# Attention probabilities transposed in 32x32 blocks by VectorE, weighted sums on four row groups of TensorE

## The reference, cut to what matters

```python
def attend(qb):                       # one block of 128 queries
    s = jnp.einsum('bqgrd,bkgd->bgrqk', qb, k).astype(jnp.float32)
    p = jax.nn.softmax(s, axis=-1).astype(v.dtype)
    return jnp.einsum('bgrqk,bkgd->bqgrd', p, v)
```

## Time and profile before

| what | value |
|---|---|
| median of 3 runs | 1152.69 us (1152.6 to 1153.32) |
| the profiled execution's own time | 1152.85 us |
| its span, first to last instruction | 1151.1 us |
| PE busy | 99% of the span |
| DVE busy | 54% |
| ACT busy | 40% |
| POOL busy | 7% |
| mean granted TensorE clock | 0.999 |

### The profile page before, as it was taken

The page is one execution under the profiler, slowest core; times in us unless marked ns, Lnnn a source line. Parts: engine busy times, 40 slices in busy tenths (PEclk is TensorE's granted clock), DMA queues, the critical chain, the costliest instruction groups (busy, mean ns, idle before and its releaser), DMA issues.

```text
span 1151.1 us, 16031 instructions
## 1 busy us (share of the span) xinstructions
PE 1142.1 (99%) x6071; PEld 922.3 (80%) x6071; DVE 620.0 (54%) x776; ACT 455.4 (40%) x682; POOL 83.6 (7%) x74
## 2 busy tenths in 40 slices
PE   9999999999999999999999999999999999999997
PEld 7888888888888777666788888888888888888886
DVE  6755555553332684444598857655455555542223
ACT  6423223232222446455767655434423223232223
POOL 0000000000001120000054320020000000000000
PEclk9999999999999999999999999999999999999999
DMA  6332232332323341211121212432232232232221
GB/s 206 110 109 91 91 109 91 99 126 101 100 86 122 131 132 60 73 56 56 55 93 57 75 56 92 165 102 100 92 110 91 91 109 90 92 105 96 92 92 73
DMA packets 31679, 111.59 MB, mean 97 GB/s; under 512 B 3984, under 2 KB 5136, under 8 KB 31376
## 3 DMA queue, kind: packets, MB, share of 16 engines
q1 hardware_dynamic: 30192, 104.11, 26.9%
q10 hardware_dynamic: 1440, 6.82, 1.6%
HBM read 105.41 MB, written 4.19 MB: 95 GB/s over the span
## 4 chain that ended last, share of the span: by engine, by line
PE 99%; DMA 0%; DVE 0%; ACT 0%; issue 0%; ACTq 0%; DVEq 0%
PE ps L1161 27%; PE ps L1163 26%; PE ps L1162 26%; PE ps L1196 3%; PE ps L1195 3%; PE ps L1197 3%; PE ps L1301 1%; PE ps L1312 1%; PE ps L1327 1%; PE ps L1456 1%; PE ps L1432 1%; PE ps L1410 0%; PE ps L1449 0%; DMA raw<-up_dram 0%; PE ps L1361 0%; PE ps L1234 0%
## 5 line engine op out<-in xcount | busy, mean ns | idle before, releaser
L1161 PE MATMUL ps<-h_hi,w_hi 128*128 128x512 f32 x1024 | 407.4, 398 | 0.0
L1163 PE MATMUL ps<-h_hi,w_lo 128*128 128x512 f32 x1024 | 399.0, 390 | 0.0
L1162 PE MATMUL ps<-h_lo,w_hi 128*128 128x512 f32 x1024 | 398.8, 389 | 0.0
L768 DVE TENSOR_TENSOR w_lo<-raw,w_hi 128x1024 fp32r<-128x1024 f32 (+2 forms) x190 | 234.4, 1236 | 191.2 <-ACT w_hi L414 185.0
L414 ACT ACTIVATE w_hi<-raw 128x1024 fp32r<-128x1024 f32 (+1 forms) x182 | 196.3, 1080 | 168.0 <-PE ps L1163 96.2
L1161 PEld LDWEIGHTS ps<-h_hi,w_hi 128*128 128x128 f32 x1024 | 192.2, 188 | 55.5 <-issue 15.6
L1162 PEld LDWEIGHTS ps<-h_lo,w_hi 128*128 128x128 f32 x1024 | 192.3, 188 | 41.4 <-issue 2.9
L1163 PEld LDWEIGHTS ps<-h_hi,w_lo 128*128 128x128 f32 x1024 | 192.2, 188 | 40.5
L484 ACT ACTIVATE g_hi<-un 128x512 f32 (+1 forms) x44 | 27.8, 632 | 250.8 <-DVE un L768 250.8
L768 DVE TENSOR_TENSOR un<-ps,rs 128x512 f32<-128x512 f32 x44 | 30.4, 691 | 122.2 <-PE ps L1163 122.2
L1161 PE MATMUL ps<-g_hi,w_hi 128*128 128x512 f32 x176 | 68.5, 389 | 0.0
(11 more groups left out here) (241 smaller groups left out, 1189.8 us busy)
## 6 DMA issues: line engine op xcount, KB each, us to landing
raw<-up_dram SPq DMA_DIRECT2D x86, 512.0 KB, 3.2
raw<-proj_dram SPq DMA_DIRECT2D x26, 512.0 KB, 3.2
raw<-down_dram SPq DMA_DIRECT2D x16, 704.0 KB, 4.0
raw<-down_dram SPq DMA_DIRECT2D x22, 512.0 KB, 3.2
raw<-gates_dram SPq DMA_DIRECT2D x16, 512.0 KB, 3.2
raw<-branch_dram SPq DMA_DIRECT2D x8, 512.0 KB, 3.2
raw<-wout_dram SPq DMA_DIRECT2D x8, 512.0 KB, 3.3
x_spill_dram<-xT ACTq DMA_DIRECT2D x1, 2048.0 KB, 7.2
```

Source lines behind the costliest of these rows:

```text
L768: return V.tensor_tensor(out, a, b, op)
L1161: T.matmul(ps[:, bank, :], w_hi[:, slot, cols], moving_hi(j), start=start and j == 0, stop=False)
L1162: T.matmul(ps[:, bank, :], w_hi[:, slot, cols], moving_lo(j), start=False, stop=False)
L1163: ins = T.matmul(ps[:, bank, :], w_lo[:, slot, cols], moving_hi(j), start=False, stop=stop and j == tiles - 1)
```

## The change

The 128x128 transposes by PE and the copies behind them go. Instead DVE transposes `prob` in 32x32 blocks within each group of 32 partitions (`prob_blocks`: one instruction of 512 elements per partition and two of 256). A block transpose leaves the queries' group of 32 where it was, so partitions 32i to 32i + 31 now hold, for queries 32i to 32i + 31, all 512 keys in 16 blocks of 32. The weighted sum therefore contracts over 32 keys at a time in each of the four row groups, with the values of every key block copied to all four groups (`v_rep`, by 32 new DMAs on SP). The result of row group i goes to PSUM bank 4 + i, and `y_hi` and `y_lo` gather it from four banks.

```diff
+BLOCK = 32
+BLOCKS = S // BLOCK
+QUADS = P // BLOCK
...
+        v_rep = [at("v_rep0", 80, [P, BLOCKS // 2, P]), at("v_rep1", 100, [P, BLOCKS // 2, P])]
...
-        UP_BANKS, RES_BANKS, MEAN_BANK, Y_BANKS = (0, 2), 4, 6, (6, 7)
+        UP_BANKS, RES_BANKS, MEAN_BANK, Y_BANK = (0, 2), 4, 6, 4
...
+                        if FIRST_ITEM <= i < FIRST_ITEM + QUADS:
+                            to = i - FIRST_ITEM
+                            if to == 0:
+                                sp.wait_ge(vn_done, 1)
+                            for half in range(2):
+                                for quad in range(QUADS):
+                                    sp.dma_start(v_rep[half][BLOCK * to:BLOCK * (to + 1), quad::QUADS, :],
+                                                 v_a[BLOCK * quad:BLOCK * (quad + 1), 2 * half:2 * half + 2, :]).then_inc(vrep_loaded, 16)
                         sp.wait_ge(lo_done, BASE[name] + i + 1)
...
-            def prob_t_copy(q):
-                act.wait_ge(pt_done, 2 * q + 1)
...
-                A(prob_t0[:, :, q % 4, :], ps[:, 4, :].rearrange("p (j c) -> p j c", c=P), ACT.Copy).then_inc(pta_done, 1)
...
+            def prob_blocks(q):
+
+                if q == 0:
+                    dve.wait_ge(spilled, 16)
+                elif q % 4 == 0:
+                    dve.wait_ge(pv_done, q // 4)
+                dve.wait_ge(pn_done, 2 * q + 1)
+                V.transpose(prob_t0[:, :, q % 4, :], prob[:, 0, :].rearrange("p (j c) -> p j c", c=BLOCK)).then_inc(pt_done, 1)
+                dve.wait_ge(pn_done, 2 * q + 2)
+                for half in range(2):
+                    V.transpose(prob_t1[half][:, :, q % 4, :],
+                                prob[:, 1, S // 2 * half:S // 2 * (half + 1)].rearrange("p (j c) -> p j c", c=BLOCK)).then_inc(pt_done, 1)
+
             def attention_step(q):
 
                 if 0 <= q - 1 < ITEMS:
-                    dve.wait_ge(pt_done, 2 * q)
...
-                    for half in range(2):
-                        V.tensor_copy(prob_t1[half][:, :, (q - 1) % 4, :],
-                                      ps[:, 5, S // 2 * half:S // 2 * (half + 1)].rearrange("p (j c) -> p j c", c=P)).then_inc(ptb_done, 1)
+                    prob_blocks(q - 1)
...
-            def prob_transposes(q):
...
             def weighted(t):
                 if t == 0:
-                    pe.wait_ge(vn_done, 1)
-                if t == 1:
+                    pe.wait_ge(vrep_loaded, 16 * 2 * QUADS * QUADS)
+                    pe.wait_ge(qeps_done, 5)
                     pe.wait_ge(vn_done, 5)
...
+                else:
+                    pe.wait_ge(yalo_done, t)
+                pe.wait_ge(pt_done, 12 * t + 12)
+                for j in range(BLOCKS):
+                    for i in range(QUADS):
+                        keys = slice(BLOCK * i, BLOCK * (i + 1))
+                        for a, rows in enumerate(head_rows):
+                            probs = prob_t1[j // 8][keys, j % 8, :, :] if a else prob_t0[keys, j, :, :]
+                            ins = T.matmul(ps[rows, Y_BANK + i, P * t:P * (t + 1)], v_rep[j // 8][keys, j % 8, rows],
+                                           probs.rearrange("p s c -> p (s c)"), start=j == 0, stop=j == BLOCKS - 1)
...
             def key_transposes(u):
                 pe.wait_ge(ke_done, u + 1)
+                if u == 0:
+                    pe.wait_ge(yalo_done, PAIRS)
```

More of the change, by code:

```diff
@@ L154, in build @@
         prob = at("prob", 76, [P, 2, S])
-        prob_t0 = nc.alloc_sbuf_tensor_at("prob_t0", [P, ST, 4, P], F32, offset=big_at + 2 * 4 * S)
-        prob_t1 = [nc.alloc_sbuf_tensor_at("prob_t1a", [P, ST // 2, 4, P], F32, offset=big_at + 6 * 4 * S),
-                   at("prob_t1b", 56, [P, ST // 2, 4, P])]
+        prob_t0 = nc.alloc_sbuf_tensor_at("prob_t0", [P, BLOCKS, 4, BLOCK], F32, offset=big_at + 2 * 4 * S)
+        prob_t1 = [nc.alloc_sbuf_tensor_at("prob_t1a", [P, BLOCKS // 2, 4, BLOCK], F32, offset=big_at + 6 * 4 * S),
+                   at("prob_t1b", 56, [P, BLOCKS // 2, 4, BLOCK])]
+        v_rep = [at("v_rep0", 80, [P, BLOCKS // 2, P]), at("v_rep1", 100, [P, BLOCKS // 2, P])]
         q_cos = prob
@@ L209, in build @@
         s_done, nm_done, p_done, pt_done = sem("s_done"), sem("nm_done"), sem("p_done"), sem("pt_done")
-        pta_done, ptb_done, pv_done = sem("pta_done"), sem("ptb_done"), sem("pv_done")
+        vrep_loaded, pv_done = sem("vrep_loaded"), sem("pv_done")
         inv_done, pn_done, yahi_done, yalo_done = sem("inv_done"), sem("pn_done"), sem("yahi_done"), sem("yalo_done")
@@ L343, in key_to_end @@
                 if u == 0:
-                    pool.wait_ge(pt_done, 2 * ITEMS)
+                    pool.wait_ge(pt_done, 3 * ITEMS)
                 else:
@@ L547, in exp_scores @@
                     if q:
-                        act.wait_ge(pt_done, 2 * q - 1 + a)
+                        act.wait_ge(pt_done, 3 * q - 2 + 2 * a)
                     A(prob[:, a, :], ps[:, 2 + a, :], ACT.Exp, bias=neg_max[:, q, a:a + 1],
@@ L558, in y_hi @@
                 act.wait_ge(pv_done, t + 1)
-                A(ya_hi[:, t, :], ps[:, Y_BANKS[t % 2], :], ACT.Copy).then_inc(yahi_done, 1)
+                A(ya_hi[:, t, :].rearrange("p (s i c) -> p s i c", i=QUADS, c=BLOCK),
+                  ps[:, Y_BANK:Y_BANK + QUADS, P * t:P * (t + 1)].rearrange("p i (s c) -> p s i c", c=BLOCK), ACT.Copy).then_inc(yahi_done, 1)
             def sigmoids():
@@ L611, in _ @@
                     y_hi(q // 4 - 1)
-                if q >= 1:
-                    prob_t_copy(q - 1)
                 if 0 <= q < ITEMS:
@@ L921, in y_lo @@
                 dve.wait_ge(yahi_done, t + 1)
-                tt(ya_lo[:, t, :], ps[:, Y_BANKS[t % 2], :], ya_hi[:, t, :].bitcast(F32), ALU.subtract).then_inc(yalo_done, 1)
+                by_quad = lambda y: y.rearrange("p (s i c) -> p s i c", i=QUADS, c=BLOCK)
+                tt(by_quad(ya_lo[:, t, :]), ps[:, Y_BANK:Y_BANK + QUADS, P * t:P * (t + 1)].rearrange("p i (s c) -> p s i c", c=BLOCK),
+                   by_quad(ya_hi[:, t, :].bitcast(F32)), ALU.subtract).then_inc(yalo_done, 1)
             def inverse_sums(q):
@@ L1333, in items @@
                     weighted((q - 2) // 4)
-                if 0 <= q - 1 < ITEMS:
-                    prob_transposes(q - 1)
                 if 0 <= q < ITEMS:
```

6 lines of the change are left out of this document (removed).

## The result

| | median | range |
|---|---|---|
| before | 1152.68 us (6 runs) | 1152.53 to 1153.32 |
| after | 1156.97 us (6 runs) | 1156.25 to 1158.22 |
| ratio | 1.0037 | 95% interval 1.0026 to 1.0047 |

The account below looks back on a forecast made before the run. PE, busy 99%, was taken as the bound, with the DVE and ACT loop 0.30 us behind and setting the pace afterwards. A gain of 3.8 us at the first HGRN2 tile, less 0.3, gave 1149.4 us, range 1141 to 1163.

Parts of the forecast that it names:

- PE, transposes: Gap between units on PE in ordinary items: from 2.26 to 1.38 us, 0.88 us off 16 times, 14.1 us off PE.
- DVE, transposes, T = 1.29: An item's three block transposes on DVE take 0.61 + 0.34 + 0.34 = 1.29 us, between 1.0 and 2.6.
- The loop of 7.75 us: Per-item loop of DVE and ACT: 6.46 us plus 1.29 us of transposes, setting the pace over PE's 6.73 us.
- SP, v = 0.63: Each of 32 new DMAs costs SP 0.63 us (0.33 to 1.26); unit 12's load 8.0 us later, first maxima 7.3 us late.
- PE itself may wait a microsecond or two: PE may wait that long for its units around the delayed loads, hidden because the loop, not PE, ends the stretch.
- The weighted sum at 3.75 us: Each weighted sum on PE: 32 steps of 0.112 us on eight places plus 0.17 us, 0.7 us more over the four.
- Can PE start records that fast?: Check on the weighted sum: 14.6 ns per record needed; 32 records in 0.46 us gave 14.4 ns at most, just met.
- The loop, not PE, ends the stretch: Attention stretch: 16 rounds of the loop, not PE, set the end of the last transposes, at 563.7 us.
- 2.3 us of cover over each sum: Slack on PE over each of the first three weighted sums, as DVE reaches item 4's transposes at 475.4, weighted(0) ends about 473.1.
- The chain of ACT and DVE: First HGRN2 tile: this chain arrives at 584.4, PE at 584.0; the later decides, 3.8 us gained, 3.5 after less slack.
- the one with small matmuls far apart: Weighted sums: small matmuls start 25 ns apart, the last sum 2.7 us longer, 1153.3 us, no difference; chance 0.06.
- Rival 2: SP's new DMAs dearer, seen at unit 12's load: slower, 1161.2 us at 1.0 us each; chance 0.24 of 0.8 or more.

Follow-up runs that it names:

- e5: The kernel after the change with half of each weighted sum left out (second 256 keys not added): 1149.98 us (one run).
- e3: The kernel after the change with each weighted sum cut in two halves, the next scores or half a gate unit between them: 1155.41 us.
- e1: The kernel after the change with the 32 v_rep DMAs behind the loads of units 13 to 18, not ahead of those of 9 to 12: 1149.71 us.
- e2: The kernel after the change with DVE's transposes ahead of split_lo, under ACT's w_hi, except for items 0, 4, 8 and 12: 1158.23 us.
- e4: The kernel before the change with its weighted sums cut into 128 matmuls of 32 columns on all 128 rows: 1169.9 us.
- e6: The kernel after the change with v_rep DMAs behind later loads, sums in halves (last in quarters), and DVE's transposes ahead of split_lo: 1146.23 us.
- e8: The kernel after the change with 25 matmuls of 32x32 (100 weight loads and matmuls) put ahead of the projection: 1157.87 us.

## Why the prediction was wrong

- *PE, transposes: 0.88 us off each of 16 items.* Right where PE ran free: the gap is 1.38 us where it was 2.26.
- *DVE, transposes, T = 1.29.* Right: 1.28. The loop of 7.75 us: 7.71.
- *SP, v = 0.63.* Nearly right: four batches of 5.16, 5.50, 5.12 and 5.13 us give 0.65. The load of unit 12 came at 433.52, forecast 431.0; 0.66 us of this lie ahead of the first copy (399.79 against 399.13), the rest is in the batches and a slow `q_swap` (3.06 us for four). From that load to the maxima 6.79 us, forecast 6.9.
- *"PE itself may wait a microsecond or two ..., under the same cover."* Wrong: it waited over 3 us, and PE had no cover afterwards. In the profiled execution its clock fell too, behind a wait of 2.28 us and one of 0.67; the forecast had named that danger and set it aside, since no gap that it expected exceeds 3 us.
- ***The weighted sum at 3.75 us.* This step failed.** Its pace was right (e5), but a term was missing: the supply of PE's instructions. The question "Can PE start records that fast?" was answered from a burst of 32 matmuls, 64 instructions with their weight loads; a sum has 512 and crosses two of the places 256 apart. The sums took 5.36, 5.12, 5.62 and 7.35 us, 8.5 us more in all. Of this 3.6 us lie open in the last sum and 1.8 us show as DVE's waits for the others: by that arithmetic 1156.8 would have been 1151.4 without them, on the faster side. No run shows this step alone with the queue at SP in place, since e3 kept the stall of the last sum.
- *"The loop, not PE, ends the stretch", with 2.3 us of cover over each sum.* Wrong for that reason: e1 and e2 show PE as the bound behind the first items. DVE waited for three of the sums (1.8 us in all), and the last sum started at 568.01, forecast 563.8, on a PE that had only just finished its units while the transposes ended at 567.55. Four items cost PE 4 x 6.74 + 5.4 = 32.4 us, the loop 4 x 7.71 + 0.60 = 31.4 and a wait: both near the edge.
- *The end.* From the forecast: 4.2 us later into the last sum (2.4 of them from the first maxima, 440.31 for 437.9, the rest the waits for sums), then 3.6 us more in it. The tile came at 591.82, forecast 584.4, and 1149.4 + 7.4 = 1156.8 us is what was measured. The chain of ACT and DVE that the forecast let decide was not the last: PE was.

Of the rivals, the one with small matmuls far apart (chance 0.06) had the right place and the wrong mechanism: it spoke of a pace between starts. By the Trainium skill ("TensorE: Matmul & The Clock Gate", section "Wait — 56ns, not 53.3ns?") some 25 ns lie between starts. This trace does not agree: eight starts lie within 0.05 us (568.01 to 568.06), 127 matmuls pass in 1.82 us, and the loss is in single stalls. Rival 2 (SP's copies dearer) was refuted in its price (0.65 us, not 0.8 or more) but not in its place: e1 shows that the queue cost 7.3 us, as much as the forecast had counted. That e1 lands at 1149.7 us, on the forecast, is chance: it drops the 7.3 us that were counted and keeps the stalls that were not.

What stays open: what delays a packet. In the stalls of 1.34 and 1.70 us of after it started 0.8 us behind the place before; in those of 2.75 and 2.33 us in e2 it started 2.2 and 1.7 us behind it, and in the stall of 2.33 us in e3's last sum 2.5 us, against 1.4 in after. What sets the even 29 ns of e4 is open too.

## What to carry to other kernels

Replacing few large instructions by many small ones has a price that no row of the old kernel shows as a wait: count the instructions of the new burst, weight loads included and not only its columns, and put other work between its parts. An edit can be read per part only if each is also run alone: here the trade of PE for DVE was good (e6 is 6.5 us faster than before) and both losses were in how it was fed. A queue of DMAs belongs behind the loads that somebody waits for, above all where PE would fall idle.

## What was not expected of the hardware

- PE ran 254 weight loads and matmuls on eight tile places in 1.82 us (7.2 ns each), but was fed only 256 in 3.73 us once the stock was used up. Stalls of up to 2.75 us came at fixed places of its list, 256 instructions or a multiple apart, and ended 1.26 to 1.54 us behind a packet of 16,384 bytes on the instruction queue.
- 128x32 matmuls with a new weight tile each start 29 ns apart (two places of 64 columns side by side, e4), while 32-row tiles on eight places started 14.3 ns apart, with four times the columns (e5, after).
- Behind a wait of 2.28 us, four small matmuls and a wait of 0.67 us PE's granted clock was 0.60 over four microseconds (0.50 in three of them); behind a wait of 1.69 us in e8 it stayed at 1.00.
- A 128x512 fp32 transpose in 32x32 blocks takes DVE 0.70 us, one of 256 columns 0.40 us; the copies of 256 columns out of PSUM took 0.41 to 0.43.
